# Both ends of a two-block transformer kernel: first loads, early function table, final norm

## What is computed

```python
def rmsnorm(x, g):                     # first thing: h = rmsnorm(x, norm_mix) @ w_in
    xf = x.astype(jnp.float32)
    xf = xf * lax.rsqrt(jnp.mean(xf * xf, axis=-1, keepdims=True) + NORM_EPS)
    return (xf * g.astype(jnp.float32)).astype(x.dtype)
...
    x = x + jnp.einsum('bsf,fd->bsd', jax.nn.silu(g) * u, w_down[l])
    return rmsnorm_2(x, final_norm)    # last thing
```

## Time and profile before

| what | value |
|---|---|
| three runs | 2820.61, 2821.12, 2832.75 us |
| the profiled execution, its own time | 2834.74 us |
| span in the profile | 2832.9 us |
| TensorE busy | 98% of the span |
| VectorE, ScalarE, GpSimd busy | 69%, 45%, 3% |
| first matmul starts | 11.69 us |
| last matmul of `d12` ends | 2814.61 us |

### The profile page before, as it was taken

The page is one execution under the profiler, slowest core; times in us unless marked ns, Lnnn a source line. Parts: engine busy times, 40 slices in busy tenths (PEclk is TensorE's granted clock), DMA queues, the critical chain, the costliest instruction groups (busy, mean ns, idle before and its releaser), DMA issues.

```text
span 2832.9 us, 40408 instructions
## 1 busy us (share of the span) xinstructions
PE 2789.0 (98%) x16804; PEld 2451.3 (87%) x16804; DVE 1953.0 (69%) x2416; ACT 1285.6 (45%) x1632; POOL 90.8 (3%) x67
## 2 busy tenths in 40 slices
PE   8999999999999999999999999999999999999997
PEld 7888998888888888888888878888898888888886
DVE  7777777766767665666566775666687757775775
ACT  5444545554545443344344544554454433443443
POOL 1000000001201000000000110000010000000002
PEclk9999999999999999999999999999999999999999
DMA  6555544346554555555555544443455555555553
GB/s 231 186 185 186 173 171 147 121 149 215 182 168 163 191 188 187 182 189 188 187 181 191 187 149 159 141 164 127 144 176 187 194 198 188 185 196 191 184 195 120
DMA packets 137622, 499.16 MB, mean 176 GB/s; under 512 B 15312, under 2 KB 16344, under 8 KB 137312
## 3 DMA queue, kind: packets, MB, share of 16 engines
q1 hardware_dynamic: 135792, 492.20, 51.8%
q10 hardware_dynamic: 1648, 4.39, 0.4%
HBM read 494.41 MB, written 2.11 MB: 175 GB/s over the span
## 4 chain that ended last, share of the span: by engine, by line
PE 95%; DVE 3%; ACT 1%; issue 0%; DMA 0%; POOL 0%; DVEq 0%; ACTq 0%
PE PS L474 95%; DVE wlo L1194 1%; ACT whi L812 1%; DVE X L1391 0%; DVE AR L1500 0%; DMA X<-in_x 0%; DVE X L1668 0%; DVE X L1626 0%; PE PS L551 0%; PE PS L635 0%; DVE H L1188 0%; ACT L792 0%; DVE AR L1509 0%; DVE AR L1446 0%; DVE AR L1177 0%
## 5 line engine op out<-in xcount | busy, mean ns | idle before, releaser
L474 PE MATMUL PS<-H,whi 128*128 128x512 f32 (+1 forms) x5472 | 1798.1, 382 | 11.8 <-DVE wlo L1194 11.7
L1194 DVE TENSOR_TENSOR wlo<-raw,whi 128x1024 fp32r<-128x1024 f32 x930 | 1130.8, 1231 | 705.4 <-ACT whi L812 701.0
L812 ACT ACTIVATE whi<-raw 128x1024 fp32r<-128x1024 f32 x930 | 972.0, 1057 | 1001.0 <-PE PS L474 984.1
L474 PE MATMUL PS<-H,wlo 128*128 128x256 f32 x5072 | 1418.1, 280 | 0.0
L474 PEld LDWEIGHTS PS<-H,whi 128*128 128x128 f32 x5472 | 1003.9, 189 | 227.0 <-issue 18.2
L474 PEld LDWEIGHTS PS<-H,wlo 128*128 128x128 f32 x5072 | 958.7, 189 | 2.0 <-issue 1.7
L474 PE MATMUL PS<-Y,whi 128*128 128x512 f32 (+1 forms) x2240 | 722.8, 378 | 1.0 <-DVE X L1626 0.8
L474 PE MATMUL PS<-Y,wlo 128*128 128x256 f32 x2048 | 571.7, 279 | 0.0
L474 PEld LDWEIGHTS PS<-Y,whi 128*128 128x128 f32 x2240 | 408.2, 188 | 85.9 <-DVE X L1626 2.0
L474 PEld LDWEIGHTS PS<-Y,wlo 128*128 128x128 f32 x2048 | 386.3, 189 | 0.2
L1500 DVE TENSOR_REDUCE AR<-PS 128x512 f32<-128x1024 f32 x140 | 171.5, 1225 | 14.6
(11 more groups left out here) (160 smaller groups left out, 967.1 us busy)
## 6 DMA issues: line engine op xcount, KB each, us to landing
raw<-in_ffn SPq DMA_DIRECT2D x528, 512.0 KB, 4.4
raw<-in_w_in SPq DMA_DIRECT2D x178, 512.0 KB, 4.4
raw<-in_w_qkv SPq DMA_DIRECT2D x96, 512.0 KB, 3.8
raw<-in_w_out SPq DMA_DIRECT2D x64, 512.0 KB, 4.3
raw<-in_w_o SPq DMA_DIRECT2D x40, 512.0 KB, 3.8
raw<-in_w_q SPq DMA_DIRECT2D x8, 512.0 KB, 3.8
raw<-in_w_k SPq DMA_DIRECT2D x8, 512.0 KB, 3.8
raw<-in_w_v SPq DMA_DIRECT2D x8, 512.0 KB, 4.6
```

What stands on the lines that cost most here:

```text
L474: return e.matmul(out, l, r, start=start, stop=stop)
L812: a.then_inc(e.activation(c.whi[:, s % NW, :], c.raw[:, s % NRAW, :], ACT.Copy), "whi")
L1194: v.then_inc(e.tensor_tensor(c.wlo[:, s % NW, :], c.raw[:, s % NRAW, :], c.whi[:, s % NW, :].bitcast(F32), ALU.subtract), "wlo")
```

## The change

`norm_mix` leaves the vector of constants and becomes the first 16 columns of the array that holds x, so that one load (from ScalarE's queue) brings both. Raw tile 0 is loaded, rounded and subtracted in two halves of 128x512, and TensorE's first four blocks wait for the first half only. The halves alternate with h0(0) and h0(1). ScalarE issues the load of the logarithm and exponential table before it waits for x. At the end, ScalarE scales each pair of slices in place by the final gain after it has squared it, for all eight tiles of `d12`, and loads the table at j = 6. The task `norm` 6 starts three slots earlier: TensorE sums `SUM` then, and `SQ[1]` three slots later. VectorE multiplies six pairs by the root, GpSimd the other two; each pair is stored by itself, the last two from ScalarE's queue.

```diff
@@ tasks
-    out += [(first_slot("g1") + 4, "norm", 5), (N_SLOT, "norm", 6)]
+    out += [(first_slot("g1") + 4, "norm", 5), (N_SLOT - 3, "norm", 6)]
@@ sync_program
-    load(0)
+    half = SUB // 2
+    e.dma_start(c.raw[:, 0, 0:half], c.d["w_in"][0][:, 0:half]).then_inc(c.sems["raw_first"], 16)
+    e.dma_start(c.raw[:, 0, half:SUB], c.d["w_in"][0][:, half:SUB]).then_inc(c.sems["raw0"], 16)
...
-    for k in range(0, 16, 4):
-        s.wait_ge("gain_x", k + 4 - k // 4 - 1)
-        s.wait_ge("pool_x", 4 + k // 4 + 1)
-        e.dma_start(c.out[:, k * T:(k + 4) * T], c.xt(k, 4)).then_inc(c.sems["out"], 16)
+    for i in range(6):
+        s.wait_ge("gain_x", i + 1)
+        e.dma_start(c.out[:, 2 * i * T:(2 * i + 2) * T], c.xt(2 * i, 2)).then_inc(c.sems["out"], 16)
@@ tensor_program, norm
+        last = norm_mm(bank, c.SUM, True, n != 6, n in (3, 4))
         if n == 6:
+            yield from idle(3)
             p.wait_ge("sq", 8 * n + 8)
-        p.then_inc(norm_mm(bank, c.SUM, c.SQ[1] if n == 6 else None, n in (3, 4)), "norm_sum")
+            last = norm_mm(bank, c.SQ[1], False, True, False)
+        p.then_inc(last, "norm_sum")
@@ tensor_program, halves
-        p.wait_ge("wlo", b // 8 + 1)
+        if b < 4:
+            p.wait_ge("wlo_first", 1)
+        else:
+            p.wait_ge("wlo", b // 8 + 1)
@@ scalar_program
+        if stage == "d12":
+            a.wait_ge(*a.at)
+            for k in (2 * j, 2 * j + 1):
+                a.then_inc(e.activation(c.xt(k), c.xt(k), ACT.Copy, scale=c.col("final_norm_2", k)), "scaled")
+            if j == 6:
+                load(LN_EXP)
...
-    e.dma_start(c.vec[:, 0:n], c.d["vec"][:, 0:n]).then_inc(c.sems["gains"], 16)
-    e.dma_start(c.xt(0, 2), c.d["x"][:, 0:2 * T]).then_inc(c.sems["x0"], 16)
-    a.wait_ge("gains", 16)
+    e.dma_start(c.XG[:, 0:16 + 2 * T], c.d["x"][:, 0:16 + 2 * T]).then_inc(c.sems["x0"], 16)
+    load(LN_EXP)
     h0(0)
+    half = SUB // 2
+    a.wait_ge("raw_first", 16)
+    a.then_inc(e.activation(c.whi[:, 0, 0:half], c.raw[:, 0, 0:half], ACT.Copy), "whi_first")
     h0(1)
+    a.wait_ge("raw0", 16)
+    a.then_inc(e.activation(c.whi[:, 0, half:SUB], c.raw[:, 0, half:SUB], ACT.Copy), "whi")
...
+    for i in (6, 7):
+        a.wait_ge("pool_x", i - 5)
+        e.dma_start(c.out[:, 2 * i * T:(2 * i + 2) * T], c.xt(2 * i, 2)).then_inc(c.sems["out"], 16)
@@ vector_program (the same order of halves at the start; then the end)
-    for k in range(16):
-        if k % 4:
-            v.then_inc(e.scalar_tensor_tensor(c.xt(k), c.xt(k), c.col("final_norm_2", k), c.RN, ALU.mult, ALU.mult), "gain_x")
+    for i in range(6):
+        v.wait_ge("scaled", 2 * i + 2)
+        v.then_inc(times(c.xt(2 * i, 2), c.xt(2 * i, 2), c.RN), "gain_x")
@@ gpsimd_program
-    g.wait_ge("sq", 56)
-    for k in range(0, 16, 4):
-        g.then_inc(e.tensor_scalar(c.xt(k), c.xt(k), c.col("final_norm_2", k), None, ALU.mult), "pool_x")
     g.wait_ge("norm_ok", 7)
-    g.wait_ge("pool_x", 4)
-    for k in range(0, 16, 4):
-        g.then_inc(e.tensor_tensor(c.xt(k), c.xt(k), c.RN, ALU.mult), "pool_x")
+    g.wait_ge("scaled", 16)
+    for i in (6, 7):
+        x = two(c.xt(2 * i, 2))
+        g.then_inc(e.tensor_tensor(x, x, both(c.RN), ALU.mult), "pool_x")
```

More of the change, by code:

```diff
@@ L298 @@
 SEMS = (
-    "pe_own act_own dve_own pool_own raw0 raw1 raw2 raw3 x0 x1 x2 x3 x4 x5 x6 x7 c1 gains vec mem c2 rel rows hank out "
+    "pe_own act_own dve_own pool_own raw0 raw1 raw2 raw3 x0 x1 x2 x3 x4 x5 x6 x7 c1 raw_first whi_first wlo_first scaled vec mem c2 rel rows hank out "
     "whi wlo sub_done acc0 acc1 h_hi h_made y_hi y_made cr "
@@ L323, in __init__ @@
         self.wlo = sb("wlo", [P, NW, SUB], F32R)
-        self.X = sb("X", [P, 16 * T])
+        self.XG = sb("XG", [P, 16 + 16 * T])
+        self.X, self.mix = self.XG[:, 16:], self.XG[:, 0:16]
         self.op = {"H": sb("H", [P, 16, 2, T], F32R), "Y": sb("Y", [P, 16, 2, T], F32R)}
@@ L460, in sync_program @@
         load(w)
-    for k in range(0, 16, 4):
-        s.wait_ge("gain_x", k + 4 - k // 4 - 1)
-        s.wait_ge("pool_x", 4 + k // 4 + 1)
-        e.dma_start(c.out[:, k * T:(k + 4) * T], c.xt(k, 4)).then_inc(c.sems["out"], 16)
-    s.wait_ge("out", 64)
+    for i in range(6):
+        s.wait_ge("gain_x", i + 1)
+        e.dma_start(c.out[:, 2 * i * T:(2 * i + 2) * T], c.xt(2 * i, 2)).then_inc(c.sems["out"], 16)
+    s.wait_ge("out", 128)
     s.wait_ge("rows", 16)
@@ L481, in take, with norm_mm @@
         return c.misc[b]
[L483 to L488, removed]
+    def norm_mm(bank, s, start, stop, cols):
+        mm(bank[:, 0:T], c.ones, s[:, 0:T], start, False)
+        last = mm(bank[:, 0:T], c.ones, s[:, T:2 * T], False, stop)
         if cols:
@@ L508, in mnorm @@
         p.wait_ge("madd", 7)
-        p.then_inc(norm_mm(bank, c.MSUM, None, True), "mnorm_sum")
+        p.then_inc(norm_mm(bank, c.MSUM, True, True, True), "mnorm_sum")
         yield
@@ L834, in norm @@
         _, r, col = norm_dst(c, n)
-        yield
+        yield from idle(3 if n == 6 else 1)
         if col is not None:
@@ L1143, in h0 @@
         a.wait_ge(f"x{k // 2}", 16)
-        a.then_inc(e.activation(c.hi("H", k), c.xt(k), ACT.Copy, scale=c.col("norm_mix", k)), "h_hi")
-    n = VOFF["norm_mix"][1]
-    e.dma_start(c.vec[:, 0:n], c.d["vec"][:, 0:n]).then_inc(c.sems["gains"], 16)
-    e.dma_start(c.xt(0, 2), c.d["x"][:, 0:2 * T]).then_inc(c.sems["x0"], 16)
-    a.wait_ge("gains", 16)
+        a.then_inc(e.activation(c.hi("H", k), c.xt(k), ACT.Copy, scale=c.mix[:, k:k + 1]), "h_hi")
+    e.dma_start(c.XG[:, 0:16 + 2 * T], c.d["x"][:, 0:16 + 2 * T]).then_inc(c.sems["x0"], 16)
+    load(LN_EXP)
     h0(0)
+    half = SUB // 2
+    a.wait_ge("raw_first", 16)
+    a.then_inc(e.activation(c.whi[:, 0, 0:half], c.raw[:, 0, 0:half], ACT.Copy), "whi_first")
     h0(1)
-    for s in range(NW):
+    a.wait_ge("raw0", 16)
+    a.then_inc(e.activation(c.whi[:, 0, half:SUB], c.raw[:, 0, half:SUB], ACT.Copy), "whi")
+    for s in range(1, NW):
+        for k in range(4 * s - 2, min(4 * s + 2, 16)):
+            h0(k)
         split(s)
-        if s < 4:
-            for k in range(4 * s + 2, min(4 * s + 6, 16)):
-                h0(k)
     a.wait_ge("vec", 16)
@@ L1221, in norm @@
         bank = c.bank("norm", n, "b")
+        if n == 6:
+            yield from idle(3)
         v.wait_ge("norm_sum", n + 1)
@@ L1225, in norm @@
         mean(c.SUM[:, 0:T], bank[:, 0:T], eps, "norm_mean")
-        yield from idle(2)
+        if n < 6:
+            yield from idle(2)
         if col is not None:
@@ L1643, in vector_program, with lo0 @@
                  "cr": cr, "mid": mid, "dfa": dfa, "dfb": dfb, "stk": stk, "bnd": bnd})
[L1645 to L1648, removed]
+    def lo0(k):
+        lo("H", k, 1, c.xt(k), c.mix[:, k:k + 1])
+    lo0(0)
+    half = SUB // 2
+    v.wait_ge("whi_first", 1)
+    v.then_inc(e.tensor_tensor(c.wlo[:, 0, 0:half], c.raw[:, 0, 0:half], c.whi[:, 0, 0:half].bitcast(F32), ALU.subtract), "wlo_first")
+    lo0(1)
+    v.wait_ge("whi", 1)
+    v.then_inc(e.tensor_tensor(c.wlo[:, 0, half:SUB], c.raw[:, 0, half:SUB], c.whi[:, 0, half:SUB].bitcast(F32), ALU.subtract), "wlo")
+    for s in range(1, NW):
+        for k in range(4 * s - 2, min(4 * s + 2, 16)):
+            lo0(k)
         split(s)
-        if s < 4:
-            for k in range(4 * s + 2, min(4 * s + 6, 16)):
-                lo("H", k, 1, c.xt(k), c.col("norm_mix", k))
     v.wait_ge("vec", 16)
```

9 lines of the change are left out of this document (4 added, 5 removed).

## The result

The change makes the kernel slower: 2841.35 us (median of nine executions, 2822.07 to 2843.26) against 2820.61 (nine, 2815.62 to 2832.75) of the kernel before beside it. The ratio is 1.0049 [1.0028 to 1.0071], the ratio of the medians alone 1.0074. The forecast was 2815.3, its range ended at 2828. The profiled execution took 2842.38, with a span of 2840.6; the one of before took 2834.74.

The account below looks back on a forecast made before the run. The chain lies 95% on TensorE; the change touches what it cannot cover, before its first and after its last matmul. Start 3.5 plus end 2.3 gives 5.8 us off the median 2821.1: 2815.3, range 2811 to 2828.

Parts of the forecast that it names:

- First matmul: Start: TensorE's first matmul at 8.1 instead of 11.69, 3.6 us earlier, with x landing at 6.2.
- the equal-landing-times reading: Start: early requests took 5.0 to 5.89 us whatever their size, so a half tile lands little quicker than a whole.
- Clock: Start: TensorE's clock rises 4.6 us after the first matmul, so the 3.6 us gain stays.
- The bound of 16.3: Start: if the clock rise stays at 16.3, 1.6 us is lost and 2.0 remains; witness, a slow 7.8 us after a pause.
- Supply: Start: VectorE's lead over TensorE at tile 3 just holds; 0.1 us taken off, no TensorE pause before 48 us.
- Sum over `SUM` ahead: End: moving these matmuls into the stream of `d12` gains nothing; 0.99 us added there and removed behind the square.
- Products: End: VectorE's six products end 5.8 us after the root, GpSimd's two take 1.9 each; gain 0.9 us (0.6 to 1.5).
- Stores: End: five pairs left after 2825.5 finish at 2830.2 against 2832.4; the stores add 0.1 us of gain.
- Table load: End: the load between mean and logarithm goes, gaining 1.28 us, with no further drain of 1.38 to win.
- (b): Rival: the body moves by itself through clock falls in shifted pauses; 2826.9 upwards, chance 0.15, or 17 us faster, 0.06.
- (a): Rival: the start gives little, x landing at 7.08 and clock rising at 16.3; gain 3.8, 2817.3 us, chance 0.15.
- (c): Rival: slower, TensorE catches up with VectorE in the first tiles, halts, and its clock stays low; chance 0.02.

Follow-up runs that it names:

- e5: The changed kernel with x, H, Y in the layout of before and the gains brought by their own load; 2823.47 us, ratio 0.9981.
- e13b: The changed kernel with x last in SBUF and the 16 columns left in the vectors, so only x is 64 bytes off; 2817.45 us, 0.9986.
- e18: e16 unchanged, repeated on another chip in more rounds; 2814.02 us, ratio 0.9970 against the kernel before.
- e15b: The changed kernel with 48 unused columns ahead of the gains and 16 back in the vectors, H, Y and all behind shifted 256 bytes; 2823.04 us, 0.9994.
- e16: The changed kernel with x last and 16 columns put ahead of `SUM`, leaving only `ones` 64 bytes lower besides x; 2814.67 us, 0.9966.
- e7: The kernel before with 256 unused bytes ahead of x, moving all buffers behind; 2833.98 us, ratio 1.0021.
- e14b: The kernel before with 128 unused bytes between x and H; 2839.01 us, ratio 1.0052.
- e9: The changed kernel with a pair of float32 128x256 matmuls inserted four times in each SwiGLU; 2848.61 us, ratio 1.0078.
- e10: The changed kernel with four different small matmuls, one of each kind, inserted in each SwiGLU; 2840.38 us, ratio 1.0045.

## Why the prediction was wrong, point by point

The step that failed is the sentence "The sum touches neither what made it long nor the body, so it comes off the median". The reuse of one load for x and the gains was costed as one request less. It also moved the moving operands of nearly all matmuls by 64 bytes, an edit costed at nothing because it issues nothing. The kernel before with 64 bytes ahead of x and no other edit (e1) loses 23 us (2846.41 against 2822.96 beside it), and the change without the shift (e5, e13b) loses none.

- **First matmul.** Forecast 8.1, measured 7.96 (and 7.91 in e18). x landed at 6.04 for 6.2, the equal-landing-times reading of the earlier trace rows held. With the gains' own load (e5) it was 9.10.
- **Clock.** Forecast a rise 4.6 us after the first matmul; it came after 3.5, so a little better. The bound of 16.3 didn't come up. (Its witness was read a little short: with 0.89 over 1668 to 1670 in the earlier trace rows the rise comes at 1668.4, 8.0 us instead of 7.8, which changes nothing.)
- **Supply.** Forecast 0.1 lost, a lead of 3.5 and no halt before 48. TensorE halts 0.37 at 13.00 and 0.50 at 33.35, and waits 0.77 instead of 0.54 at the next stretch, which starts at 56.44: the lead is 2.82 (59.26 - 56.44), of 3.73. These three are 1.1, so this term was mis-sized by itself, without the layout. In e18 the halts are 0.37 and 0.35 and the stretch starts at 55.66, a lead of 3.60; its 47 blocks up to 54.42 go at 346.5 against 353.5, which is 0.3 of the difference.
- **Sum over `SUM` ahead.** Forecast 0 and got less. The four records left took 1.82 for 0.99, with the clock fallen to 0.50 behind a pause of 2.2; in the eleven other profiles with this end they took 1.14 to 1.24, and in e18 the clock was 1.00. So the 1.82 belongs to this one execution, and the term is otherwise right. The forecast had no term for such a fall.
- **Products.** Forecast 5.8 for VectorE's six pairs, and 1.9 for each of GpSimd's; measured 5.83 (2831.87 to 2837.70) and 1.74. The longest of VectorE's took 1749 ns beside GpSimd, the usual one 685.
- **Stores.** Forecast the end 2.8 us behind the last product; it came 2.9 behind (2840.6 - 2837.7). The stretches 2837 to 2838 and 2838 to 2839 moved 381 and 389 GB/s, near the 406 of the earlier trace rows. The Trainium skill (DMA: Bandwidth & Descriptors, section Measured) has 341 for loads of a mebibyte; these stores of 256 KB did better.
- **Table load.** 1.28 gone, nothing more. The Trainium skill (ScalarE: Activation LUTs, section What ACT_TABLE_LOAD costs) would have given a further 1.38; no run here shows it.
- **Sum.** 5.8 forecast. In a layout without the shift, group against group, the whole change gives 3.0 to 5.9 (e5, e13b, e15b), 5.3 in e16 and 7.4 in e18. So the terms of both ends were right within about 3 us. In the profile of the changed kernel they add up to 4.7: the lead of 2.82, and 2.8 at the end less the 0.9 that moved into the stream. In that of e18 they add up to 6.2 (3.60 and 2.6). The 5.8 lies between, partly by luck: more was lost in the supply than forecast, and the clock and, in e18, the end gave more.
- **The rivals.** (b), the body moves by itself, was given 0.15 upwards and 2826.9. Its mechanism, the clock's falls in pauses, is not what happened: the granted clock is 1.00 all through the stretches that got longer. It had the witness in hand, runs 12 us apart with no change, and priced only one such step. There are two SwiGLUs and the early stages: in before one step at most is common, in the changed kernel two steps together are (six of nine executions). (a) and (c) didn't come.

The account of the two profiles: 3.7 earlier at the first matmul, of which 0.9 is gone by 56; 3.0, 2.1 and 14.0 longer in three of the long stretches; the stages between these shorter by 5.8 in all (92.8 to 91.2, 102.8 to 100.5, 389.3 to 387.3); 2.8 at the end. That makes 7.7, the difference of the spans. Of the 5.8 between the stretches 1.6 is the stream of three-matmul blocks, 353.4 ns for 360.0; the rest (2.2 and 2.0) was not looked into.

What stays open is what inside TensorE's reads makes the paces, why 16 columns ahead of `SUM` matter, and what the draw of an execution is: e7 and e15b have the same shifts, and e7 had nine of twelve in slower groups, e15b six.

## What to carry to other kernels

An edit that adds a few columns to a buffer moves every buffer behind it, and that is an edit of all instructions that read these: list the new addresses, and measure that shift alone, as e1 does. In this kernel the `H` and `Y` of the matmul stream may move by 16384 bytes, or by 256 (e15b; with the same shifts e7 was slow more often), but not by 64 or 128, and the small matmuls' operand not by 64; whether 256 would do elsewhere no run shows. When a change moves the time with no wait to show for it, compare the lengths of TensorE's unbroken stretches and the start-to-start time of equal blocks, since a busy share of 100% at clock 1.00 hides two per cent. Spread between executions is a finding too: distances that repeat (here 13 to 14 us, 9 in the shifted layout) belong to a stage, and they say what that stage can do on its own.

## What the runs showed of the hardware

- A stream of pairs of matmuls (128x512 and 128x256, rounded float32) runs at 346.7 or 353.3 ns a pair with its moving operands where they were or 256 bytes further, at 348.8 or 353.3 with 64 bytes of shift, and at 351.1 with 128. Nothing waits, and the granted clock is 1.00. The Trainium skill (TensorE: Matmul & The Clock Gate, section Back-to-back issue gap) has, for a matmul without its weight load, the columns over 2.4 GHz and 2.5 ns, from which I estimate 325 for a pair; every pace here is longer. No run here shows what the 22 ns above it are.
- A block of three matmuls of 256 columns goes the other way: 360.0 ns with its operands in place, 353.4 with 64 bytes of shift, 356 with 128 (11.52, 11.31 and 11.40 us for 32 blocks in before, after and e14b).
- The pace holds for hundreds of microseconds and changes at a small float32 matmul (2088.30 in the kernel before, 1026.52 in e9, 1474.49 and 2675.41 in e10). The address of that matmul's moving operand counts.
- TensorE's clock fell to 0.50 in the microseconds after the pause of 2.2 us at the end, in the changed kernel; in e18, behind a pause as long, it stayed at 1.00 and the same four records took 1.15 instead of 1.82.
